# Second block of a two-block transformer kernel: norms done for 128 tokens at a time, between the products around them

## The reference, cut to what matters

```
h = rms_norm(x, g_mix[L]);   q, k, v = split(h @ w_in[L])        # 1024 -> 3 x 1024
x = x + concat(differential, moba, dilated attention) @ w_out[L]  # 16 heads
h = rms_norm(x, g_ffn[L])
x = x + (silu(conv3(h @ w_up)[gate]) * conv3(h @ w_up)[val]) @ w_down[L]   # 1024 -> 2 x 2816 -> 1024
```

## Time and profile before

| what | value |
|---|---|
| three runs | 4088.11, 4095.9, 4098.93 us |
| profiled execution, as timed | 4092.97 us |
| its span | 4090.9 us |
| TensorE busy (matmul) | 3694.2 us, 90% |
| VectorE, ScalarE, POOL busy | 29%, 17%, 12% |
| granted TensorE clock, mean | 0.964 of full |

### The profile page before, as it was taken

The page is one execution under the profiler, slowest core; times in us unless marked ns, Lnnn a source line. Parts: engine busy times, 40 slices in busy tenths (PEclk is TensorE's granted clock), DMA queues, the critical chain, the costliest instruction groups (busy, mean ns, idle before and its releaser), DMA issues.

```text
span 4090.9 us, 33008 instructions
## 1 busy us (share of the span) xinstructions
PE 3694.2 (90%) x12728; PEld 1773.9 (43%) x12728; DVE 1193.1 (29%) x2725; ACT 714.1 (17%) x1454; POOL 491.3 (12%) x437
## 2 busy tenths in 40 slices
PE   6899988899999887888888888999999999999998
PEld 3355554444444433333233334544444445444443
DVE  2336655634210220211110124442221134422211
ACT  2023333222310200000000012321110113221100
POOL 1003333412100000000000001101220011012200
PEclk8899998899999999999999999999999999999999
DMA  7322222211213479999999981012122210122220
GB/s 249 124 81 68 80 71 85 75 34 59 78 62 103 171 282 409 409 409 409 409 409 409 409 341 52 31 42 82 62 83 77 77 52 31 42 81 64 82 77 31
DMA packets 301577, 634.08 MB, mean 155 GB/s; under 512 B 32435, under 2 KB 145699, under 8 KB 301167
## 3 DMA queue, kind: packets, MB, share of 16 engines
q1 hardware_dynamic: 239904, 591.96, 38.5%
q10 hardware_dynamic: 61519, 40.02, 3.5%
HBM read 625.50 MB, written 10.24 MB: 155 GB/s over the span
## 4 chain that ended last, share of the span: by engine, by line
PE 51%; DMA 18%; DVE 3%; ACT 1%; SPq 1%; issue 1%; POOL 0%; DVEq 0%; ACTq 0%
PE psum L295 28%; PE psum L2704 7%; DMA arena<-in_w_exp_up_dram 7%; DMA arena<-in_w_exp_gate_dram 7%; PE psum L1491 6%; DMA arena<-in_w_exp_down_dram 4%; PE psum L2292 3%; PE psum L1319 2%; PE psum L1347 1%; PE psum L1328 1%; PE psum L2241 1%; SPq L264 1%; PE psum L307 0%; PE psum L2210 0%; DVE arena L1425 0%
## 5 line engine op out<-in xcount | busy, mean ns | idle before, releaser
L295 PE MATMUL psum<-arena 128*128 128x512 f32 (+1 forms) x3392 | 1383.2, 566 | 6.5 <-POOL arena L1882 2.4
L295 PEld LDWEIGHTS psum<-arena 128*128 128x128 f32 x3392 | 646.2, 192 | 729.5 <-issue 703.4
L2292 PE MATMUL psum<-arena 128*64 128x512 f32 x3072 | 696.3, 598 | 150.2 <-DMA arena<-in_w_exp_up_dram 78.8
L2292 PEld LDWEIGHTS psum<-arena 128*64 128x64 f32 x3072 | 234.1, 137 | 593.6 <-issue 573.1
L1491 PE MATMUL psum<-arena 128*128 128x512 f32 x768 | 354.7, 617 | 0.8 <-DVE arena L521 0.8
L2704 PE MATMUL psum<-arena 128*128 128x512 f32 x704 | 303.0, 592 | 0.0
L710 PE MATMUL psum<-arena 128*128 128x512 f32 (+1 forms) x768 | 270.6, 512 | 1.3 <-ACT arena L533 1.3
L1491 PEld LDWEIGHTS psum<-arena 128*128 128x128 f32 x768 | 148.2, 197 | 193.1 <-issue 191.2
L1425 DVE CUSTOM_DVE_ANT_0 arena<-psum,arena 128x512 f32<-128x512 f32 (+3 forms) x224 | 114.0, 546 | 394.0 <-PE psum L1319 386.2
L2747 POOL TENSOR_SCALAR arena<-arena 128x512 f32<-128x512 f32 x88 | 137.8, 1566 | 718.2 <-ACT arena L2726 718.2
L2704 PEld LDWEIGHTS psum<-arena 128*128 128x128 f32 x704 | 133.3, 189 | 169.4 <-issue 169.4
(11 more groups left out here) (269 smaller groups left out, 2818.4 us busy)
## 6 DMA issues: line engine op xcount, KB each, us to landing
arena<-in_w_exp_gate_dram SPq DMA_DIRECT2D x128, 1024.0 KB, 18.5
arena<-in_w_exp_up_dram SPq DMA_DIRECT2D x128, 1024.0 KB, 18.7
arena<-in_w_exp_down_dram SPq DMA_DIRECT2D x128, 1024.0 KB, 18.6
arena<-in_w_in_dram SPq DMA_DIRECT2D x64, 1024.0 KB, 5.2
arena<-in_w_up_dram SPq DMA_DIRECT2D x88, 512.0 KB, 4.7
arena<-in_w_ada_dram SPq DMA_DIRECT2D x24, 1024.0 KB, 7.5
arena<-in_w_down_dram SPq DMA_DIRECT2D x20, 1024.0 KB, 5.0
arena<-acs_scratch ACTq DMA_DIRECT2D x64, 256.0 KB, 3.6
```

The source lines that it names most:

```text
L295: mm = pe.matmul(shaped(b, l, r), l, r, start=kt == 0, stop=kt == nkt - 1)
L2292: mm = pe.matmul(banks[n][64 * j:64 * j + 64, :], lhs[:, kt, 64 * j:64 * j + 64], w, start=kt == 0, stop=kt == 2 * nkb - 1)
```

## The change

All of it is in the second block. The tile helpers of layer 0's first norm are used for the four other norms as well.

- End of attention and norm ahead of the MLP (both layers): `pe_last_out_2` does the last `w_out` product tile by tile (left and right half of a tile one after the other) and puts in the transposes of tile i-2 after tile i; `pe_up_first` does the first up group in two passes of 256 tokens (128x256 matmuls, twice as many), with the transposes of tiles 2 and 3 between the banks of the first pass. The second pass waits for tiles 2 and 3.
- Between the layers: the second half of `w_down` goes one tile at a time (`pe_down_tile`: 22 weight slices for one bank, then the next bank), the norm follows tile by tile, and layer 1 begins with its value product (v before q and k, on SP's queue also).
- End: `w_down`'s second half by tiles too; each tile is normed and stored in two halves of 128x512, so 8 DMAs of 256 KB.
- ScalarE preloads the function table that holds both Ln and Exp at the start of `act_between` and of `act_end`. The load of `g_final` moves up to the end of layer 1's attention, ahead of the MLP on ScalarE's queue. `xa` is gone (`xnb` is used), and buffers behind it move.

The diff, cut to its core:

```diff
+        def pe_last_out_2(pe, L):
+            for j in (6, 7):
+                pe.wait_ge(*at("oT2", L, j))
+            for i in range(4):
+                for half in range(2):
+                    nm = ("wo", L, 6, half)
+                    b = open_bank(pe, (nm, i), PALL)
+                    if i == 0:
+                        pe.wait_ge(*at("wfull", (nm, 0)))
+                    for kt in range(2):
+                        mm = pe.matmul(b, oT2[:, 6 + kt, i * 128:(i + 1) * 128], wt(nm, kt, 512), start=kt == 0, stop=kt == 1)
...
+                if i > 1:
+                    pe_tile_turn(pe, ("f", L), i - 2, xnb, (PALL, PALL))
+        def act_last_out_2(act, L):
+            nm = ("f", L)
+            for i in range(6):
+                if i > 1:
+                    act_tile_cols(act, nm, i - 2, 1, HT2, mlp_scale(L), None)
+                if i < 4:
+                    act_tile_sums(act, nm, X, i, junk3)
+                if 0 < i < 5:
+                    act_tile_rows(act, nm, X, i - 1, xnb)
+        def dve_last_out_2(dve, L):
+            for i in range(6):
+                if i < 4:
+                    for half in range(2):
...
+                        dve.tensor_tensor(d, PS.of(key), d, ALU.add).then_inc(*up(S("dve_X"), ("free", key), ("X", nm, i, half)))
+                if i > 1:
+                    dve_tile_cols(dve, nm, i - 2, 0, HT2, mlp_scale(L), None)
+                if 0 < i < 5:
+                    dve_tile_rows(dve, nm, X, i - 1, xnb)
+        def pe_up_first(pe, L):
+            banks = [open_bank(pe, (nm, i), PALL) for i in range(4)]
+            for t in range(2):
+                for i in range(4):
+                    if t == 0 and 0 < i < 3:
+                        pe_tile_turn(pe, ("f", L), i + 1, xnb, (PALL, PALL))
+                    for kt in range(8):
...
+                            for x in (2 * t, 2 * t + 1):
+                                pe.wait_ge(*at("HT", ("f", L), x, kt // 4))
+                        mm = pe.matmul(banks[i][:, 256 * t:256 * t + 256], wt(nm, kt, 512)[:, i * 128:(i + 1) * 128], HT2[:, kt, 256 * t:256 * t + 256], ...
+        def pe_down_tile(pe, L, i):
+            nm = ("dn", L, 1)
+            b = open_bank(pe, (nm, i), PALL)
+            for kt in range(22):
+                if i == 0 and kt % 4 == 0:
+                    pe.wait_ge(*at("wfull", (nm, kt // 4)))
+                mm = pe.matmul(b, actT[:, kt, i * 128:(i + 1) * 128], wt(nm, kt, 512), start=kt == 0, stop=kt == 21)
...
+        def pe_between(pe):
+            nm, v = ("a", 1), pe_v_2(pe, 1, 0, PALL)
+            for i in range(4):
+                pe_down_tile(pe, 0, i)
+                if i:
+                    pe_tile_turn(pe, nm, i - 1, xnb, (PALL, PALL))
+            pe_first_2(pe, 1, nm, v, (0, 1))
+            pe_tile_turn(pe, nm, 3, xnb, (PALL, PALL))
+            pe_first_2(pe, 1, nm, v, (2, 3))
+        def act_between(act):
+            act.preload_act_table_set(LNEXP)
+            for i in range(4):
+                act_tile_sums(act, nm, X, i, junk3, (0,))
+            for i in range(4):
+                act_tile_sums(act, nm, X, i, junk3, (1,))
+                act_tile_rows(act, nm, X, i, xnb)
+                if i:
+                    act_tile_cols(act, nm, i - 1, 1, HT2, attn_scale(1), None)
...
+        def dve_end(dve):
+            for i in range(4):
+                dve_down(dve, 1, 0, i, "end")
+            for i in range(4):
+                dve_down(dve, 1, 1, i, "end")
+                dve_tile_root(dve, "end", i)
...
+                for h in range(2):
+                    dve.scalar_tensor_tensor(out=ob[:, i, HALF[h]], in0=X[:, i, HALF[h]], scalar=col(rx, i), in1=gf[:, HALF[h]], op0=ALU.mult,
+                                             op1=ALU.mult).then_inc(*up(S("dve_ob"), ("ob", i, h)))
```

More of the change, by code:

```diff
@@ new lines, in pe_mlp @@
+            nm = ("dn", L, 0)
+            banks = [open_bank(pe, (nm, i), PALL) for i in range(4)]
+            for g in range(6):
+                nk = 4 if g < 5 else 2
+                pe.wait_ge(*at("wfull", (nm, g)))
+                pe.wait_ge(*at("act", L, min(4 * g + 3, 21)))
+                for i in range(4):
+                    for kt in range(4 * g, 4 * g + nk):
+                        mm = pe.matmul(banks[i], actT[:, kt, i * 128:(i + 1) * 128], wt(nm, kt, 512), start=kt == 0, stop=kt == 21)
+                    keys = [("full", (nm, i))] if g == 5 else []
+                    if i == 3:
+                        keys.append(("wfree", (nm, g)))
+                    if keys:
+                        mm.then_inc(*up(S("pe_down"), *keys))
@@ new lines, in dve_between @@
+        def dve_between(dve):
+            nm = ("a", 1)
+            for i in range(4):
+                dve_down(dve, 0, 0, i, nm)
+            for i in range(4):
+                dve_down(dve, 0, 1, i, nm)
+                dve_tile_rows(dve, nm, X, i, xnb)
+                if i:
+                    dve_tile_cols(dve, nm, i - 1, 0, HT2, attn_scale(1), None)
+            dve_v_2(dve, 1, 0, 0)
+            dve_tile_cols(dve, nm, 3, 0, HT2, attn_scale(1), None)
+            dve_v_2(dve, 1, 0, 2)
+            run(dve_qk_2(dve, 1, 0))
+            dve_rope_2(dve, 1, 0, 3)
@@ L2764, in dve_down, with act_end @@
+        gf, ob = sb(DSLOT + 320, 1024), xnb
+        def act_end(act):
+            act.preload_act_table_set(LNEXP)
             for half in range(2):
                 for i in range(4):
-                    key, d = (("dn", L, half), i), X[:, i, half * 512:half * 512 + 512]
-                    dve.wait_ge(*at("full", key))
-                    dve.tensor_tensor(d, PS.of(key), d, ALU.add).then_inc(*up(S("dve_X"), ("free", key), ("Xd", L, half, i)))
-        def act_x_sums(act, key, names):
+                    act_tile_sums(act, "end", X, i, junk3, (half,))
@@ L2783, in sp_program, with sp_end @@
+        def sp_end(sp):
+            for i in range(4):
+                for h in range(2):
+                    sp.wait_ge(*at("ob", i, h))
+                    sp.dma_start(out[0, i * 128:(i + 1) * 128, HALF[h]], ob[:, i, HALF[h]]).then_inc(*up(S("out_done"), ("out", i, h), by=16))
+            sp.wait_ge(*at("out", 3, 1))
         def sp_program(sp):
@@ L2809, in sp_program @@
                 sp_mlp(sp, L)
[L2810 to L2813 removed]
+            sp_end(sp)
         def pe_program(pe):
```

208 lines of the change are left out of this document (92 added, 116 removed).

## The result

Four runs of the changed kernel had a median of 4055.93 us (4051.33 to 4059.24), four of the kernel before beside them 4096.1 us: a ratio of 0.9904, interval 0.9887 to 0.9921. The profiled execution took 4055.48 us, of which the span is 4053.7, where before it was 4092.97 and 4090.9. The forecast was 4056.

A forecast was written before the change was run, and what follows sets the result against it. TensorE's chain of waits bounds the kernel, with 57.4 us in four gaps. Gains 8.3 + 10.6 + 10.8 + 6.7 + 1.6 = 38.0 us off 4092.97 give 4055.0, taken as 4056; own range 4050 to 4062, 8 in 10 4048 to 4069.

The forecast's parts named there:

- A: Layer 0, last w_out product through first up group: 54.5 us would become 46.2, a gain of 8.3 us.
- C: Layer 1, last w_out product through first up group: 56.8 us to 46.2, gain 10.6, as two table loads go.
- B: Between layer 0's down product and layer 1's projections: of 14.5 us only 3.7 of transposes stay, gain 10.8 us.
- rival 3: Down's second half: weights come late if a load takes five times as long; gain about 18 us, 4075; chance 0.02.
- D: From the last down product to the span's end: 14.1 us would become 7.4, a gain of 6.7 us (6.3 to 7.7).
- T: End of down's last product; VectorE's last output was forecast 4.4 us after it, the kernel's end 7.4 us after.
- Layer 1's attention: Norm of the differential heads: its two table loads of 1.28 us go, gain 1.6 us (bounds 0 and 2.6).
- The sum: All five gains, two norms ahead of MLPs, between layers, end, layer 1's attention: 38.0 us off the profiled 4092.97.
- (1): Tile chains take 6.5 us a tile: 11 us less gain over both norms ahead of the MLP, 4066; chance 0.14.
- (2): Clock falls to 1.2 of 2.4 GHz in interleaved stretches: all at half costs 73 us, 4128; chance 0.04.
- (4): No gain: TensorE's idle time only moves from the gaps into the streams behind them; chance 0.02.

The follow-up runs named there:

- the order without waits: Final experiment: changed kernel with tile 1's transposes, VectorE's bank emptying and ScalarE's scaling reordered in the norm ahead of the MLP; 4050.88 us, again 4046.51.
- the one with the 3.3 us wait: Changed kernel with down's second half as before (four banks together, blocks in the outer loop), norms still by tiles; 4063.72 us, ratio 0.9936.

## Why the prediction was right

**A and C** were 8.5 and 10.8 against 8.3 and 10.6. The length after, 46.2, is the forecast's to the tenth, and the waits are where it put them. That it is right to the tenth is luck: the work was 44.9 (the order without waits), not 45.2, since eight transposes take 0.87 us and not 0.93, and the waits cost 1.3, not 1.0. The 0.2 too little in both is in the lengths before, 54.7 and 57.0 by the timeline where the count had 54.5 and 56.8. That the split is free, which was only read off 64 records, is shown over 2816.

**B** was 11.1 against 10.8, with no wait; the difference is again the transposes, 4 x 0.87 in place of 4 x 0.93. Its cover is shown: taken away, it costs 6.3 us. The weights (rival 3) never came late: no bracket of the down product names a DMA.

**D** was 7.2 against 6.7. VectorE's last output came at T + 4.4 as forecast; the term that was mis-sized is the tail behind it. A store of 256 KB lands in 2.0 us where one of 512 KB took 2.8, so the tail is 6.9 - 4.4 = 2.5, not 3.0. One thing in D was right by its total only: the early load of `g_final` was priced as an issue, but its absence costs 1.1 us, as the kernel with the preload alone showed.

**Layer 1's attention.** The wait behind the differential heads' norm is 2.12 us where it was 3.75 (TensorE's timeline, after):

```profile
3368.97 0.41 PE L1333 MATMUL psum<-arena 128*128 128x128 f32 x2 [2.12 <-DVE arena L1437]
```

Over the whole stretch TensorE's brackets sum to 24.8 us before and 22.9 after, in layer 0 to 22.9 both times. The loads so cost 1.9 us of waiting, near the 1.6. But that the stage became 1.7 shorter doesn't prove it: layer 0's, whose code and waits are the same, became 1.6 shorter too. In the preload alone, layer 1's stage kept its length, 272.5, with the 1.9 us of waits gone: TensorE was busy 1.8 us longer, at a mean clock of 0.944 and not 0.950. The kernel without the preloads is the cleaner comparison: there the waits are back (24.8 us), busy time (247.8 us) and clock (0.950) are those of the changed kernel, and the stage is 1.9 longer. So at the same clock the term is worth its wait of 1.9 us; what a single execution shows of it depends on the clock (last section).

**The sum** was 38.0 against 37.2 of span (37.5 of the execution), and this agreement is better than that of the stages. Those that the change touches gave some 39.5. The two that it doesn't touch gave +4.1 and -1.6. The 4.1 us lie in the first block: its last stretch of experts began 4.1 us later. In the twelve executions profiled, all with this same first block, layer 0's first score was between 2497.9 and 2507.6 us, and three executions of the changed kernel itself had 2497.9, 2506.3 and 2507.6. So the 4.1 us are the spread of executions and not the change, and that they brought the sum nearer to the forecast is chance. The 1.6 us of layer 0's attention are spread too (last section).

**Rivals.** (1), chains of 6.5 us a tile, is refuted: two waits of 0.85 us in sum, not 6.5. Its length did appear in the kernel without the split (6.2 us of waits), where nothing stood beside the chains. (2), the lower clock, is refuted for this kernel by 1.00 in the interleaved stretches, but the mechanism is real, as that kernel and the one with the 3.3 us wait showed. (4), gaps that only move, is refuted by the 37 us. The Trainium skill (ScalarE: Activation LUTs, What ACT_TABLE_LOAD costs) was weighed for the loads, at 2.66 us a switch: by that price one pair would hold ScalarE for 5.3 us, an estimate from the page. The rows above agree with the 1.28 us that it gives the load by itself, not with the drain of 1.38 that it adds: the two loads and the ACTIVATE behind the first run from 3580.17 to 3583.05, with 0.01 to 0.02 us between a load and the next instruction. They agree with its advice (Table sets) on the set that holds both Ln and Exp.

## What to carry to other kernels

A norm between two products is worth tiling when each tile's chain (here 3.0 us to the root, 4.3 in series with its outputs) has at least as long a piece of the neighbouring product beside it; order that product so that its tiles finish apart, not together, and find the first work behind the norm that needs only part of the rows: without that work A gained nothing at all. Before tiling a step, count what is paid once per step and will be paid per tile: a function table load of 1.28 us went from one pair to four. And when a wait is taken away, look for the one that it hid, such as a late load of a small operand.

## What the runs showed of the hardware that was not expected

The same attention code takes different times, by when the granted clock falls. Two executions of the kernel of the last experiment (stretch, us, PE, PEld, DVE, ACT, POOL, clock, DMA share, GB/s), the second run's layer 0 and the first run's layer 1:

```profile
2504.06:2771.69 267.63, 244.51 (x918) 130.44 (x918) 120.10 (x426) 76.30 (x219) 32.51 (x28) 0.96 0.11 36
```

```profile
3299.89:3575.07 275.18, 252.57 (x917) 134.40 (x917) 120.15 (x426) 76.41 (x219) 32.47 (x28) 0.93 0.11 35
```

The instructions and the work of the other engines are the same, and TensorE's idle time nearly so (23.1 and 22.6 us, the length less the busy time); TensorE's busy time differs by 8.1 us, at a clock of 0.96 and 0.93. Over all the kernels and both layers the stage lay between 267.6 and 275.3 us. Of the stage's 27 slices of 10 us, four executions had clocks below 1.00 in slices 2 to 9 and again in 18 to 22, each in others of them. What places the falls is open. It follows that a saving of 2 us inside such a stretch can't be read from its length, only from its waits, or from executions with the same busy time, while the ten up groups and half of down, without a wait, took 350.9 to 351.0 us in both layers, before and after.
